# Where the stationary operands of a fused two-block kernel lie, relative to the streamed weights, modulo 512 bytes

## The reference

```python
proj = jnp.einsum('bsd,de->bse', h, w_in[l])                 # 2048 -> 6152
x = x + jnp.einsum('bse,ed->bsd', mixed, w_out[l])           # 2048 -> 2048
u = jax.nn.relu(jnp.einsum('bsd,df->bsf', h2, w_up[l]))      # 2048 -> 8192
x = x + jnp.einsum('bsf,fd->bsd', u * u, w_down[l])          # 8192 -> 2048
...
proj = xn @ w_in[l]                                          # 2048 -> 7184
h = h + mix @ w_out[l]                                       # 2048 -> 2048
qry = jnp.einsum('td,dhk->thk', xt, w_query)                 # 2048 -> 2048
hid = jax.nn.gelu(jnp.einsum('pd,phkd->phk', xb, u_tab[eb])) # table: 16384 x 2048
y = jnp.einsum('phk,phkd->pd', gb * hid, v_tab[eb])          # table: 16384 x 2048
```

## Time and profile before

| what | us |
|---|---|
| median of 2 runs | 3210.43 |
| the profiled execution's span | 3209.0 |
| PE (matmul) busy | 3191.6 (99%) |
| PEld (weight load) busy | 2854.0 (89%) |
| DVE busy | 2030.1 (63%) |
| ACT busy | 1447.3 (45%) |
| POOL busy | 496.9 (15%) |

### The profile page before, as it was taken

The page is one execution under the profiler, slowest core; times in us unless marked ns, Lnnn a source line. Parts: engine busy times, 40 slices in busy tenths (PEclk is TensorE's granted clock), DMA queues, the critical chain, the costliest instruction groups (busy, mean ns, idle before and its releaser), DMA issues.

```text
span 3209.0 us, 48201 instructions
## 1 busy us (share of the span) xinstructions
PE 3191.6 (99%) x19975; PEld 2854.0 (89%) x19975; DVE 2030.1 (63%) x1837; ACT 1447.3 (45%) x1271; POOL 496.9 (15%) x418
## 2 busy tenths in 40 slices
PE   9999999999999999999999999999999999999999
PEld 7888899999999888888989999999999888888887
DVE  5455665556555667765476888999975555555554
ACT  5454453333433364464444444555544433334333
POOL 0000000000000002136200002888840000000000
PEclk9999999999999999999999999999999999999999
DMA  7444565555555453342255566677676656556563
GB/s 282 165 159 158 172 225 194 196 186 193 195 187 193 158 183 119 132 158 105 93 211 204 199 216 222 224 251 251 229 263 259 241 225 261 228 230 257 226 261 118
DMA packets 129572, 644.18 MB, mean 201 GB/s; under 512 B 12672, under 2 KB 45840, under 8 KB 60304
## 3 DMA queue, kind: packets, MB, share of 16 engines
q1 hardware_dynamic: 95792, 623.03, 53.3%
q10 hardware_dynamic: 33632, 18.99, 1.9%
HBM read 606.31 MB, written 35.66 MB: 200 GB/s over the span
## 4 chain that ended last, share of the span: by engine, by line
PE 97%; DVE 1%; ACT 1%; DMA 0%; SPq 0%; issue 0%; DVEq 0%; ACTq 0%
PE pj L305 12%; PE pj L304 12%; PE pj L306 12%; PE pj L282 7%; PE pj L281 7%; PE pj L280 7%; PE pj L1774 4%; PE pj L1772 4%; PE pj L890 4%; PE pj L892 4%; PE pj L1773 4%; PE pj L891 4%; PE pm L282 2%; PE pt L282 2%; PE pt L281 2%; PE pm L281 2%
## 5 line engine op out<-in xcount | busy, mean ns | idle before, releaser
L262 ACT ACTIVATE hi<-raw 128x2048 fp32r<-128x2048 f32 x534 | 1023.8, 1917 | 1372.7 <-PE pj L306 640.7
L269 DVE TENSOR_TENSOR lo<-raw,hi 128x2048 fp32r<-128x2048 f32 x400 | 918.5, 2296 | 677.5 <-ACT hi L262 676.7
L304 PE MATMUL pj<-xh,hi 128*128 128x256 f32 x3328 | 919.9, 276 | 0.0
L305 PE MATMUL pj<-xl,hi 128*128 128x256 f32 x3328 | 918.8, 276 | 0.0
L306 PE MATMUL pj<-xh,lo 128*128 128x256 f32 x3328 | 918.8, 276 | 0.0
L305 PEld LDWEIGHTS pj<-xl,hi 128*128 128x128 f32 x3328 | 625.0, 188 | 0.6
L304 PEld LDWEIGHTS pj<-xh,hi 128*128 128x128 f32 x3328 | 624.8, 188 | 0.6
L306 PEld LDWEIGHTS pj<-xh,lo 128*128 128x128 f32 x3328 | 624.8, 188 | 0.0
L269 DVE TENSOR_TENSOR lo_in<-raw,hi 128x2048 fp32r<-128x2048 f32 x134 | 308.1, 2300 | 268.9 <-ACT hi L262 268.4
L2495 POOL TENSOR_SCALAR hotA<-cst,slotT 128x128 fp32r<-128x128 f32 x256 | 337.9, 1335 | 462.0 <-ACT slotT L2333 425.4
L1772 PE MATMUL pj<-hi,xh 128*128 128x512 f32 x576 | 232.3, 403 | 0.0
(11 more groups left out here) (408 smaller groups left out, 4243.8 us busy)
## 6 DMA issues: line engine op xcount, KB each, us to landing
raw<-w_peer SPq DMA_DIRECT2D x256, 1024.0 KB, 6.3
raw<-w_mlp SPq DMA_DIRECT2D x128, 1024.0 KB, 4.8
raw<-w_in SPq DMA_DIRECT2D x102, 1024.0 KB, 4.8
raw<-w_out SPq DMA_DIRECT2D x32, 1024.0 KB, 4.8
raw<-w_q SPq DMA_DIRECT2D x16, 1024.0 KB, 4.9
act_scratch<-hidU SPq DMA_DIRECT2D x32, 512.0 KB, 3.0
gates_scratch<-stage ACTq DMA_DIRECT2D x8, 2048.0 KB, 17.5
hidV<-act_scratch SPq DMA_DIRECT2D x32, 512.0 KB, 3.7
```

Of the source, the lines that this page charges most:

```text
L262: nc.scalar.activation(hi[:, j, :], raw[:, j, :], ACT.Copy).then_inc(hi_ready, 1)
L269: nc.vector.tensor_tensor(low(q)[:, j, :], raw[:, j, :], hi[:, j, :].bitcast(F32), ALU.subtract).then_inc(lo_ready, 1)
L304: nc.tensor.matmul(o, hi[:, j, cols], xh[:, k0 + k, :], start=clears, stop=False, skip_group_check=True)
L305: nc.tensor.matmul(o, hi[:, j, cols], xl[:, k0 + k, :], start=False, stop=False, skip_group_check=True)
```

## The change

The stationary operands of the 512 column form are moved to addresses that differ from the streamed weights by an odd multiple of 32 bytes modulo 512. `xh` and `xl` each get two names over the same memory, 32 bytes apart: `xh_up`, `xl_up` at the old remainder (192) for the 256 column form, and `xh_tok`, `xl_tok` at 224 for the 512 column form and for the tail products. The pair of one name is never in use together with that of the other: each lift (the transposed activations' copy into `xh` and `xl`) goes to the pair that the product behind it reads, by its number `n`. Buffer 0 of the coefficient copies goes to remainder 32, buffer 1 to 480; both the high and the low copy of one buffer have the same remainder. The area behind `xl` starts 1024 bytes later, and the small tile `dn` of the delta layer moves into the tail's area, over `wtail_s`. The programs of the five engines hold the same instructions, in the same order and with the same waits, as before; only addresses differ.

```diff
+TOK_SHIFT = 32
+COEF_REST = (32, 480)
...
         at_x = cursor[0]
-        xh = sb("xh", [P, KT, TT * P], F32R)
-        xl = sb("xl", [P, KT, TT * P], F32R)
+        xh_up = sb("xh_up", [P, KT, TT * P], F32R)
+        xh_tok = sb("xh_tok", [P, KT, TT * P], F32R, at=at_x + TOK_SHIFT)
+        cursor[0] += 512
+        at_xl = cursor[0]
+        xl_up = sb("xl_up", [P, KT, TT * P], F32R)
+        xl_tok = sb("xl_tok", [P, KT, TT * P], F32R, at=at_xl + TOK_SHIFT)
+        cursor[0] += 512
...
-        coef_h = [y(f"coef_h{i}", [P, 4, TT * P], F32R) for i in range(2)]
-        coef_l = [y(f"coef_l{i}", [P, 4, TT * P], F32R) for i in range(2)]
+        coef_h = [y(f"coef_h{i}", [P, 4, TT * P], F32R, rest=(at_raw + COEF_REST[i]) % 512) for i in range(2)]
+        coef_l = [y(f"coef_l{i}", [P, 4, TT * P], F32R, rest=(at_raw + COEF_REST[i]) % 512) for i in range(2)]
...
+        def stationary(n):
+            return (xh_up, xl_up) if n in (2, 5) else (xh_tok, xl_tok)
+
         def lift_act(act, n, b, gain, free=None):
+            xh, _ = stationary(n)
...
-                        nc.tensor.matmul(pair[:, t, :], xh[:, k0 + kk, tok], hi[:, j, cols], start=begin, stop=False)
-                        nc.tensor.matmul(pair[:, t, :], xh[:, k0 + kk, tok], lo_in[:, j, cols], start=False, stop=False)
-                        mm = nc.tensor.matmul(pair[:, t, :], xl[:, k0 + kk, tok], hi[:, j, cols], start=False, stop=end)
+                        nc.tensor.matmul(pair[:, t, :], xh_tok[:, k0 + kk, tok], hi[:, j, cols], start=begin, stop=False)
+                        nc.tensor.matmul(pair[:, t, :], xh_tok[:, k0 + kk, tok], lo_in[:, j, cols], start=False, stop=False)
+                        mm = nc.tensor.matmul(pair[:, t, :], xl_tok[:, k0 + kk, tok], hi[:, j, cols], start=False, stop=end)
...
-        dn = z("dn", [P, 3, TT, H])
+        dn = sb("dn", [P, 3, TT, H], at=at_tail + 4 * KT * 16)
...
-        cV_h = [y(f"cV_h{i}", [P, 4, TT * P], F32R) for i in range(2)]
-        cV_l = [y(f"cV_l{i}", [P, 4, TT * P], F32R) for i in range(2)]
+        cV_h = [y(f"cV_h{i}", [P, 4, TT * P], F32R, rest=(at_raw + COEF_REST[i]) % 512) for i in range(2)]
+        cV_l = [y(f"cV_l{i}", [P, 4, TT * P], F32R, rest=(at_raw + COEF_REST[i]) % 512) for i in range(2)]
```

More of the change, by code:

```diff
@@ L303, in multiply_up @@
                     clears = first and k == 0 and b % 2 == 0
-                    nc.tensor.matmul(o, hi[:, j, cols], xh[:, k0 + k, :], start=clears, stop=False, skip_group_check=True)
-                    nc.tensor.matmul(o, hi[:, j, cols], xl[:, k0 + k, :], start=False, stop=False, skip_group_check=True)
-                    mm = nc.tensor.matmul(o, lo[:, j, cols], xh[:, k0 + k, :], start=False, stop=end and b % 2 == 1, skip_group_check=True)
+                    nc.tensor.matmul(o, hi[:, j, cols], xh_up[:, k0 + k, :], start=clears, stop=False, skip_group_check=True)
+                    nc.tensor.matmul(o, hi[:, j, cols], xl_up[:, k0 + k, :], start=False, stop=False, skip_group_check=True)
+                    mm = nc.tensor.matmul(o, lo[:, j, cols], xh_up[:, k0 + k, :], start=False, stop=end and b % 2 == 1, skip_group_check=True)
             mm.then_inc(pe_used, 1)
@@ L507, in lift_dve @@
         def lift_dve(dve, n, b, gain):
+            xh, xl = stationary(n)
             dve.wait_ge(tp_h, 4 * n + b + 1)
@@ L518, in first_lift_act @@
             for k in range(4 * b, 4 * b + 4):
-                ins = nc.scalar.activation(xh[:, k, :], xT[:, k, :], ACT.Copy, scale=small[:, S_GATTN + k:S_GATTN + k + 1])
+                ins = nc.scalar.activation(xh_tok[:, k, :], xT[:, k, :], ACT.Copy, scale=small[:, S_GATTN + k:S_GATTN + k + 1])
             ins.then_inc(tp_h, 1)
@@ L578, in parts_pe @@
                         tok = slice(t * P, (t + 1) * P)
-                        nc.tensor.matmul(pair[:, t, :], xh[:, 4 * j + k, tok], hi[:, j, cols], start=j == 0 and k == 0, stop=False)
-                        nc.tensor.matmul(pair[:, t, :], xh[:, 4 * j + k, tok], lo_in[:, j, cols], start=False, stop=False)
-                        mm = nc.tensor.matmul(pair[:, t, :], xl[:, 4 * j + k, tok], hi[:, j, cols], start=False, stop=False)
+                        nc.tensor.matmul(pair[:, t, :], xh_tok[:, 4 * j + k, tok], hi[:, j, cols], start=j == 0 and k == 0, stop=False)
+                        nc.tensor.matmul(pair[:, t, :], xh_tok[:, 4 * j + k, tok], lo_in[:, j, cols], start=False, stop=False)
+                        mm = nc.tensor.matmul(pair[:, t, :], xl_tok[:, 4 * j + k, tok], hi[:, j, cols], start=False, stop=False)
             mm.then_inc(pe_used, 1)
```

12 lines of the change are left out of this document (6 added, 6 removed).

## The result

The changed kernel takes 3252.4 us, median of 2 runs (3252.12 and 3252.69), against 3210.43. The ratio is 1.013, with a 95% interval of 1.0113 to 1.0146: slower by 1.3%, clear of the measurement's noise (the interval reaches 0.17% to each side, not the 2% that the prediction took as the edge of what can be told). The forecast was 3143 us. The profiled execution's span is 3250.7 us against 3209.0, 41.7 us more.

A forecast was written before the change was run, and what follows sets the result against it. PE's product pace was taken to bound the kernel: 3209.0 us of span less 69.3 for 512 column products plus 2 uncovered gave 3141.7; with the runs' median 1.4 us over the span, 3143 us. The range was 3106 to 3213.

The forecast's parts named there:

- What bounds the kernel: Whole kernel: PE busy 3191.6 of 3209.0 us, waits 9.4 us, so only the pace of TensorE's products sets the time.
- Can an address matter at all?: Tail products: reads of load and stream affect each other, by some 3.5 ns per 256 columns.
- the two tail runs: Tail products before the change: 116.9 ns each with 8 and 16 stationary columns, 113.4 with 16 and 32.
- The price of a wide product: 7872 products of 512 columns: 219.9 ns each instead of 228.7, saving 69.3 us.
- The other yardstick: Plain float32 products of 256 columns: 217.5 ns a pass with a full load, used as bound from below.
- The 256 form: 0: 9984 products of 256 columns: their tiles keep their remainders, so their 113.2 ns pace changes by 0.
- What is uncovered in block 2: Block 2, 1360 to 1440 us: the ACT and DVE chain takes back 2 us of the saving, some nine chunks there.
- The lifts, `dn` and the copies: ScalarE and VectorE write the same elements 32 bytes further on, with no wait or DMA added: 0.
- C: Loads beside 512 column streams touch one line more: 3.5 to 7.0 ns a product, 3238 to 3265 us; chance 0.11.
- Rival A: 512 column products lose their whole 15.4 ns surplus: 3125 us at 217.5 ns, 3093 at 213.3; chance 0.25.

The follow-up runs named there:

- The widths: Streams of wide products alone, without the model, at widths from 512 to 224 columns and four stationary offsets; 512 columns took 226.7 to 233.4 ns, 256 took 113.3 to 120.0.
- the map: A kernel of products alone, without the model, at chosen offsets between load and stream; 512 columns took 226.7 to 234.3 ns at multiples of 32, 256 columns 113.3 to 120.0.

## Why the prediction was wrong

**What bounds the kernel** was right: PE, at its pace, with waits of 9.4 us. Nothing but the pace changed.

**"Can an address matter at all?"** Right, and so was the use of starts instead of durations. That the two tail runs differ by the place of their operands was an inference, since their loads differ too; with the moving tiles at offset 0 they take 114.1 and 113.8 ns, which supports it. The rule of the Trainium skill against it (TensorE: Matmul & The Clock Gate, "What happens when you issue a matmul"; SBUF — State Buffer, "Who interferes with whom"), by which a load takes nothing from the stream and TensorE waits for nobody, would have left 3210 us. The product streams alone, with no other engine's work in them, move from 226.7 to 234.3 ns by the offset alone; the measurement decides.

**The price of a wide product** is the step that failed: 219.9 ns taken, 233.2 measured, a saving of 8.8 ns that was a loss of 4.1. It was put together as 113.2 for the half of the stream that has the load beside it and 106.7 for a half that runs free, on the reading that one product of 512 columns should be no dearer than two of 256. The widths show why that is wrong: from 320 columns up the surplus is 13.3 ns or more at every offset tried, and the narrow form of this kernel, at 6.7, is the exception, a favourable state at its offset of 192 (at the other offsets tried it costs 117.8 to 120.0, and two such products cost more than a wide one). The yardstick was the one lucky number of the trace. The wide form had 15.4 of surplus by the prediction's count, and at most 2.2 ns of it could be had by any offset tried. Nor was there a reason in the trace why an odd multiple of 32 should be the offset that frees it: at 224 the streams alone give 233.4, the dear side of the map. The other yardstick, 217.5 ns for a pass of plain float32, is a pass of another kind and was never reached by fp32r at 512 columns.

**"The 256 form: 0"** failed as well. The tiles kept their offset, and 13 stages of 192 products went from 113.4 to 117.8 nonetheless: 10.4 us, a quarter of the loss. The prediction treated the pace as a function of the products' own addresses, and missed that the narrow one is carried over from what ran ahead.

**What is uncovered in block 2** (2 us) never arose, since the products became no faster, and PE's waits went from 9.4 to 8.1 us; so the term was not put to the test. Its count was off as well: 98 products of L1772 stand in 1360 to 1440 us, 8 to a chunk, so some twelve chunks pass there and not nine. The lifts, `dn` and the copies show no cost, as said: the sum above leaves 0.3 us. The lower end of the range, called half way between 3125 and 3093, is 3109 and not 3106.

**The rivals.** C, the new offset is worse, is what happened, at 0.11. Its price of 3.5 to 7.0 ns a product, taken from the tail's two runs, held the 4.1 measured, and its 3238 to 3265 us held the result. That is in part luck: nothing measured ties the tail's difference to the wide products' loss, and 10.4 us of the result came from narrow products that C left alone. Its reason, a slice that starts on an odd multiple of 32 and touches one line more, did not hold: the kernel moved by 32 bytes as a whole is as fast as before. Rival A (the whole surplus goes) was ruled out by the streams, in which the best of all combinations is 226.7; the figure of 216 ns from the Trainium skill (TensorE: Matmul & The Clock Gate, "Back-to-back issue gap"), which the section gives as the gap of a single warm matmul of 512 columns taken alone, was not reached by fp32r products with a load each, and the 131 ns that it gives for a stream of loads and matmuls still less. The range ended at 3213, just above "nothing happens", and so left out the side on which the truth lay: the evidence at hand was only that offsets matter, which spoke for a loss as much as for a gain.

## What to carry to other kernels

When TensorE's products with their loads follow each other without a gap, read their pace from starts, and measure the pace against the offset between stationary and moving tile in a stream of its own before laying out memory: one short kernel gave the whole map, and for the wide products it fitted the real one to 0.1 ns. For the narrow ones it had to hold the stage ahead as well. Do not infer a free surplus from the cheapest form in the same trace, since that form may sit in a favourable state that others cannot reach. A layout must be judged over the stages behind it too: at 0, the wide products won 15 us and the narrow ones behind them lost 12.

## What the runs showed of the hardware that was not expected

- The pace of fp32r products of 512 columns with a load of 128 columns each depends on the offset of the stationary tile from the moving one, with a period of 256 bytes: 226.7 ns at 0, 228.9 at 192, 232.4 at 128, 233.3 at 64, 233.4 to 234.3 at odd multiples of 32.
- At 256 columns the order of the offsets is another: 113.3 ns at 64, 117.8 at 192, 118.4 at 32, 120.0 at 0. From 320 to 384 columns the offset does nothing, and a product costs its columns' time and 13.3 ns.
- Narrow products at this kernel's offset have two stable paces, 113.3 and 117.8 ns, for the same instructions and addresses. Which one they take depends on what ran ahead, and holds for the whole stage; it can reach back over a wide stage of 96 products. At a narrow offset of 320, and for wide products at 192, no second pace was seen. A single transpose between them can change it: 11 of 12 stages turned in one layout, 7 of 12 in another, there in strict alternation.
- Below 32 bytes the place itself matters: both operands at 16 ran at 230.0 ns, both at 0, 32 or 64 at 226.7.
- What in the array or the memory produces these states was not tested; the runs show when they occur, not what they are.
